# A fifth expert slot, laid over the modulated rows and their transposes, with the expert loop written out

## The reference, cut to what matters

```
e_w = e_prob / jnp.sum(e_prob, axis=-1, keepdims=True) * g_prob
combine = jnp.sum(jax.nn.one_hot(e_global, N_EXPERTS) * e_w[..., None], axis=1)
a = jnp.einsum('nd,edf->nef', t, w_g)        # 32 x 1024 x 256, f32
u = jnp.einsum('nd,edf->nef', t, w_u)        # 32 x 1024 x 256
act = jax.nn.silu(a) * u * combine[..., None]
y = jnp.einsum('nef,efd->nd', act, w_d)      # 32 x 256 x 1024
```

## Time and profile before

| what | value |
|---|---|
| median of the 3 runs | 1055.72 us (1053.0 to 1059.05) |
| the profiled execution, its own time | 1053.05 us |
| its span, first to last instruction | 1051.2 us |
| mean granted TensorE clock | 0.91 |
| PE busy | 832.2 us, 79% |
| DVE busy | 329.7 us, 31% |
| HBM traffic | 315.82 MB read, 26.80 MB written |

### The profile page before, as it was taken

One profiled execution on the slowest core, in us unless ns is written; L12 is line 12 of the kernel. 1 busy time (PEld: TensorE's weight loads), 2 busy tenths in 40 slices (PEclk: granted clock), 3 DMA queues, 4 the chain that ended last, 5 costly groups with the idle time before them and its releaser, 6 DMA issues.

```text
span 1051.2 us, 13810 instructions
## 1 busy us (share of the span) xinstructions
PE 832.2 (79%) x4921; PEld 438.8 (42%) x4922; DVE 329.7 (31%) x803; ACT 166.2 (16%) x354; POOL 159.0 (15%) x245
## 2 busy tenths in 40 slices
PE   3899999988976889787778937997599878797740
PEld 2556565655473333333323325664433323232310
DVE  3013555555852111111111147347411110111117
ACT  1122222242001011101111012201101111101110
POOL 1032030311102021111011101001201111111010
PEclk9999999999976999999889977998599998999985
DMA  9993653295397498999999889554569999999831
GB/s 337 365 361 109 217 175 125 81 360 206 92 398 321 178 370 334 419 420 420 419 420 396 329 301 375 194 207 183 227 273 419 420 421 421 419 413 418 357 132 72
DMA packets 90242, 318.11 MB, mean 303 GB/s; under 512 B 13150, under 2 KB 26174, under 8 KB 65624
## 3 DMA queue, kind: packets, MB, share of 16 engines
q1 hardware_dynamic: 70016, 274.60, 66.1%
q0 software_dynamic: 13376, 22.16, 6.1%
q10 hardware_dynamic: 6808, 20.79, 5.2%
HBM read 315.82 MB, written 26.80 MB: 326 GB/s over the span
## 4 chain that ended last, share of the span: by engine, by line
PE 48%; DMA 35%; DVE 8%; issue 4%; ACT 2%; SPq 2%; POOL 1%; ACTq 0%; DVEq 0%; POOLq 0%
DMA ring<-in_w_expert_up 24%; PE psum L919 16%; PE psum L802 8%; PE psum L748 7%; DMA ring<-in_w_ada 6%; PE psum L941 4%; PE psum L697 3%; DMA arena<-h_scratch,gidx 2%; PE psum L906 2%; DMA arena<-y_scratch 1%; PE psum L774 1%; SPq L366 1%; PE psum L1088 1%; PE psum L853 1%; PE psum L831 1%
## 5 line engine op out<-in xcount | busy, mean ns | idle before, releaser
L919 PE MATMUL psum<-ring,arena 128*64 128x512 f32 x1088 | 268.0, 649 | 54.6 <-DMA ring<-in_w_expert_up 50.6
L919 PEld LDWEIGHTS psum<-ring,arena 128*64 128x64 f32 x1088 | 95.0, 149 | 223.8 <-issue 221.7
L941 PE MATMUL psum<-ring,arena 128*64 128x512 f32 x544 | 124.2, 598 | 30.9 <-DVE arena L1663 29.5
L1659 DVE TENSOR_TENSOR arena<-arena,psum 128x256 f32<-128x256 f32 x34 | 14.3, 422 | 311.6 <-ACT arena L1212 311.6
L802 PE MATMUL psum<-ring,hT 128*128 128x384 f32 x288 | 97.9, 494 | 0.0
L941 PEld LDWEIGHTS psum<-ring,arena 128*64 128x64 f32 x544 | 39.7, 136 | 92.0 <-issue 76.6
L578 POOL DMA_INDIRECT y_scratch<-arena,sidx x34 | 34.5, 1014 | 255.3 <-DVE arena L1669 255.3
L748 PE MATMUL psum<-ring,hT 128*128 128x512 f32 x160 | 69.5, 593 | 1.1 <-ACT hT L1285 0.7
L697 PE MATMUL psum<-ring,silu 128*32 128x128 f32 x1536 | 52.7, 296 | 21.5 <-DMA ring<-in_w_ada 21.2
L802 PEld LDWEIGHTS psum<-ring,hT 128*128 128x128 f32 x288 | 54.3, 194 | 34.9 <-issue 1.4
L1669 DVE COPY arena<-psum 128x512 f32<-128x512 f32 x34 | 23.5, 692 | 132.6 <-PE psum L941 132.6
(11 more groups left out here) (177 smaller groups left out, 780.4 us busy)
## 6 DMA issues: line engine op xcount, KB each, us to landing
ring<-in_w_expert_gate SPq DMA_DIRECT2D x64, 1024.0 KB, 12.7
ring<-in_w_expert_up SPq DMA_DIRECT2D x64, 1024.0 KB, 19.5
ring<-in_w_expert_down SPq DMA_DIRECT2D x64, 1024.0 KB, 21.2
ring<-in_w_ada SPq DMA_DIRECT2D x24, 2048.0 KB, 15.7
ring<-in_w_qkv SPq DMA_DIRECT2D x9, 1024.0 KB, 12.4
arena<-m_scratch POOLq DMA_DIRECT2D x12, 512.0 KB, 7.4
h_scratch<-h ACTq DMA_DIRECT2D x6, 1024.0 KB, 10.6
arena<-y_scratch ACTq DMA_DIRECT2D x6, 1024.0 KB, 7.9
```

The source lines that it names most:

```text
L919: last = pe.matmul(bank[b][64 * e:64 * e + 64, :].rearrange("p (g n) -> p g n", g=2), mem.GT[b][:, c, 64 * e:64 * e + 64], w, start=(c == ...
L941: last = pe.matmul(bank[5 + half][64 * e:64 * e + 64, :], mem.actT[b][:, f, 64 * e:64 * e + 64], w[:, f, 512 * half:512 * half + 512], sta ...
```

## The change

`SLOTS` becomes 5. The ring keeps four slots; the fifth, `last_slot`, is one allocation in which `h` and `hT` lie side by side. Expert e goes to slot e modulo 5. The fifth slot's load (expert 4) is issued behind the loads of the first four, once the logits are done and `h_out` says that all rows are in HBM. After `gate_up` of pair n, SP now issues experts 2n + 5 and 2n + 6 (only expert 31 for n = 13). As the last pairs now sit in other slots, `ada` units 6 to 8, 10 and 11 of layer 1 move to A0 to A2, the second projection to B0 and B1, unit 9 to B2; and in layer 1 experts 2 and 3 are loaded first, 0 and 1 after the projection.

The loops over pairs are written out on all engines, so each has 16 copies of `first` and 16 of `body` per layer, and both packed words are read ahead of them. The gather and the `gt` past the end and the `landing` transfer are gone, and the fixed addresses no longer come from registers.

```
-SLOTS = 4
+SLOTS = 5
...
+SLOT_OF = [e % SLOTS for e in range(EXPERTS)]
...
-        self.ring = sb("ring", [P, SLOTS, SLOT])
+        self.ring = sb("ring", [P, (SLOTS - 1) * SLOT])
...
-        self.h = sb("h", [P, TILES, D])
-        self.hT = sb("hT", [P, KC, TOK])
+        self.last_slot = sb("h_hT", [P, SLOT])
+        self.h = self.last_slot[:, 0:TILES * D].rearrange("p (t n) -> p t n", t=TILES)
+        self.hT = self.last_slot[:, TILES * D:].rearrange("p (k n) -> p k n", k=KC)
...
+    def slot(self, e):
+        i = SLOT_OF[e]
+        return self.last_slot if i == SLOTS - 1 else self.ring[:, SLOT * i:SLOT * i + SLOT]
...
         def passes(eng, l, S, first, body):
-            eng.wait_ge(words_done, l + 1)
-            with eng.Fori(0, 2) as half:
-                word = eng.value_load(mem.words[0:1, bass.ds(half, 1)], min_val=0, max_val=(1 << 24) - 1)
-                with eng.Fori(0, PAIRS // 4) as it:
-                    for b in range(2):
...
+            word = words(eng, l)
+            for n in range(PAIRS):
+                first(n, n % 2)
+                times = times_of(eng, word, n)
+                with eng.If(times > 0):
+                    with eng.Fori(0, times) as r:
+                        body(n, n % 2, r + 1, eng.snap(further[eng]))
+                        eng.reg_add(further[eng], further[eng], 1)
...
+            def load_last_slot(l):
+                sp.wait_ge(logits_ps, l + 1)
+                sp.wait_ge(h_out, 16 * TILES * (l + 1))
+                load_expert(l, SLOTS - 1)
...
             for e in (2, 3):
                 load_expert(0, e)
+            load_last_slot(0)
...
+                for n in range(PAIRS):
...
+                    coming = [e for e in (2 * n + SLOTS, 2 * n + 1 + SLOTS) if e < EXPERTS]
+                    if coming:
+                        sp.wait_ge(main[l]["u_ps"], n + 1)
+                        sp.wait_ge(gate_up_through, all_done)
+                        for e in coming:
+                            load_gate_up(l, e)
+                        sp.wait_ge(main[l]["d_ps"], n + 1)
+                        sp.wait_ge(down_through, all_done)
+                        for e in coming:
+                            load_down(l, e)
...
-                    for e in range(2):
+                    for e in (2, 3):
                         load_expert(1, e)
                     sp.wait_ge(proj_ps, 12)
-                    for e in range(2, 4):
+                    for e in (0, 1):
                         load_expert(1, e)
+                    load_last_slot(1)
...
-                pool.dma_start(mem.landing[l:l + 1, :], A["k_rows"][0:1, 0:P]).then_inc(S["scattered"], 16)
...
-                    gt(S, n + 1, 16 * it + (16, 32)[b], 1 - b)
+                    if n + 1 < PAIRS:
+                        gt(S, n + 1, 16 * ((n + 1) // 2 + 1), 1 - b)
```

More of the change, by code:

```diff
@@ L68 @@
     LANDED[_unit] = _sum[_place]
+SLOT_OF = [e % SLOTS for e in range(EXPERTS)]
+LOAD_OF = {}
+for _l in range(2):
+    for _e, _s in enumerate(SLOT_OF):
+        LOAD_OF[_l, _e] = _l * SLOT_OF.count(_s) + SLOT_OF[:_e + 1].count(_s)
 _C = {}
@@ L436, in _ @@
                 load_expert(0, e)
+            load_last_slot(0)
             for l in range(2):
-                sp.wait_ge(words_done, l + 1)
-                for half in range(2):
-                    word = sp.value_load(mem.words[0:1, half:half + 1], min_val=0, max_val=(1 << 24) - 1)
-                    with sp.Fori(0, PAIRS // 4 - half) as it:
-                        for b in range(2):
-                            n = half * (PAIRS // 2) + it * 2 + b
-                            times = sp.snap((word >> (it * 6 + 3 * b)) & 7, min_val=0, max_val=PASSES - 1)
-                            first_done = sp.snap(n + 1)
-                            sp.reg_add(further[sp], further[sp], times)
-                            all_done = sp.snap(further[sp])
-                            slots = [2 * b + e for e in range(2)]
-                            experts = [sp.snap(2 * n + 4 + e) for e in range(2)]
-                            sp.wait_ge(main[l]["u_ps"], first_done)
-                            sp.wait_ge(gate_up_through, all_done)
-                            for e in range(2):
-                                load_gate_up(slots[e], l, experts[e])
-                            sp.wait_ge(main[l]["d_ps"], first_done)
-                            sp.wait_ge(down_through, all_done)
-                            for e in range(2):
-                                load_down(slots[e], l, experts[e])
@@ L671, in _ @@
-                pool.wait_ge(S["scattered"], 16 * PAIRS + 16)
+                pool.sem_inc(S["o_free"], 2)
+                word = words(pool, l)
+                for n in range(PAIRS):
+                    b = n % 2
+                    times = times_of(pool, word, n)
+                    pool.wait_ge(S["gt_ps"], n + 1)
+                    with pool.If(times > 0):
+                        gather(extra, l, PAIRS + n, pool.snap(further[pool]), 2)
+                    if n + 2 < PAIRS:
+                        gather(S, l, n + 2, n + 2, b)
+                    if n >= 1:
+                        pool.wait_ge(S["scattered"], 16 * n)
+                        pool.sem_inc(S["o_free"], 1)
+                    scatter(S, l, n, n, b)
+                    with pool.If(times > 0):
+                        pool.wait_ge(S["scattered"], 16 * n + 16)
+                        with pool.Fori(0, times) as r:
+                            k = pool.snap(further[pool])
+                            k16 = pool.snap(16 * k + 16)
+                            with pool.If(r > 0):
+                                gather(extra, l, (r + 1) * PAIRS + n, k, 2)
+                            pool.sem_inc(extra["o_free"], 1)
+                            scatter(extra, l, (r + 1) * PAIRS + n, k, b)
+                            pool.wait_ge(extra["scattered"], k16)
+                            pool.sem_inc(turns, 1)
+                            pool.reg_add(further[pool], further[pool], 1)
@@ L939, in down @@
                         for e in range(2):
-                            w = mem.ring[:, slots[e], 4 * D:].rearrange("p (k n) -> p k n", k=2)
+                            w = mem.slot(2 * n + e)[:, 4 * D:].rearrange("p (k n) -> p k n", k=2)
                             last = pe.matmul(bank[5 + half][64 * e:64 * e + 64, :],
@@ L947, in mlp, with first @@
                 S = main[l]
[L949 to L953 removed]
+                def first(n, b):
+                    pair = (2 * n, 2 * n + 1)
+                    gate_up(S, n, n, [(landed[SLOT_OF[e]], 32 * LOAD_OF[l, e]) for e in pair])
+                    if n + 1 < PAIRS:
+                        gt(S, n + 1, 16 * ((n + 1) // 2 + 1), 1 - b)
                     act_transposes(S, n, b)
[L955 removed]
+                    down(S, n, n, [(down_landed[SLOT_OF[e]], 16 * LOAD_OF[l, e]) for e in pair])
                 def body(n, b, r, k):
[L958 to L960 removed]
+                    pe.wait_ge(S["gt_act"], min(n + 2, PAIRS))
+                    pe.wait_ge(S["gt_dve"], min(n + 2, PAIRS))
                     gt(extra, k, 16 * k + 16, 2)
[L962 removed]
+                    gate_up(extra, k, n, [])
                     act_transposes(extra, k, b)
@@ L965, in body @@
                     pe.wait_ge(S["o_dve"], n + 2)
-                    down(extra, k, b, slots, [])
+                    down(extra, k, n, [])
                 gt(S, 0, 16, 0)
```

120 lines of the change are left out of this document (41 added, 79 removed).

## The result

The changed kernel takes 1042.62 us, median of four runs (1041.58 to 1043.62); the kernel before takes 1054.36 us in the runs beside it. The ratio is 0.9902 with a 95% interval of 0.9877 to 0.9928, so 8 to 13 us are gone. The profiled execution took 1042.36 us (span 1040.5) against 1053.05 (1051.2): 10.7 us less, where I had forecast 8.4.

What follows compares the result with a forecast made beforehand. Bytes through a full DMA queue at 420 GB/s were taken to bound both expert stages. Layer 0's -5.05 and layer 1's -3.35 us made -8.4, from the 1055.72 us median to 1047.3 us; range 1041 to 1056 us.

Steps and rivals of the forecast that it cites:

- What bounds it: Both expert stages: the DMA queue is full, so bytes at 420 GB/s set the pace and TensorE has slack.
- The fifth slot, -5.0 us per layer: Expert plateaus: one gate and one up load less ahead of the last gate-up block, 2.50 us each.
- The first gather, +1.0 us: Start of layer 1's expert stage: the added load delays the first gather by 1.0 us, between nothing and 2.7 us.
- half of what is left: Layer 1's first gather: queues alternate, so it waits a fair share of the load's remaining 2.7 us, taken as 1.0.
- Code, +1.0 us per layer: Expert stages: written-out TensorE code needs 12.8 more fetches per layer, spread evenly over 16 DMA engines, costing 1.0 us.
- the rival with one DMA engine behind by 11 us per layer: Expert stages: all added code fetches fall on one DMA engine, 16 us of its time per layer; slower, chance 0.09.
- The rival's second road: Each pair's `If`: a taken branch outside resident code fetches first; must exceed a few us of load wait; no separate chance.
- The `gt` past the end, -0.35 us per layer: Last pair of each layer: dropping VectorE's needless copy saves 0.35 us, between zero and 0.69 us.
- Between the layers, -0.7 us: Layer 0's end: one expert issue less ahead of the `ada` loads beside the last scatter, worth 0 to 2.5 us.
- my own signs of being wrong: Time wrong if first-to-last gate-up interval grows, layer 1's first gather far exceeds 4.4 us, or last blocks take 8.7.
- Given back by the clock and the gather: Two slow last blocks cost 3.4 us and the gather 2.0 instead of 1.0: 1051.7 us, chance 0.19.
- Less lag: Stage ends: the slowest DMA engine holds up the last block 2.5 us less per layer: 1042.3 us, chance 0.08.

Runs made afterwards that it cites:

- e4: Changed kernel with two more never-entered copies of the overflow pass in TensorE's code for each pair: 1075.50 us, 1.0222 of the kernel before.
- e1: Changed kernel with four slots and the old order of places and loads, loops still written out: 1049.39 us, 0.9961 of the kernel before.
- e2: Changed kernel with the fifth slot's load (expert 4) issued only after gate-up of pair 0: 1050.23 us, 0.9963 of the kernel before.
- e6: e1 with two gathers per layer and one `gt` past the end put back: 1051.52 us, 0.9985 of the kernel before.
- e7: Changed kernel with one more never-entered copy of the overflow pass in TensorE's code for each pair: 1043.04 us, 0.9900 of the kernel before.
- a2: Changed kernel run and profiled again, nothing altered: 1043.11 us, 0.9908 of the kernel before.
- e5: Changed kernel with gate and up of expert 31 queued ahead of expert 30's down matrix in each layer: 1039.43 us, 0.9873 of the kernel before.

## Why the prediction came out right

**What bounds it** held. Both expert stages are timed by bytes. The distance follows the bytes that stand in the queue ahead of pair 14's block and nothing else that I varied there, save e4's code.

**The fifth slot, -5.0 us per layer:** 4.8 us in layer 1 and 5.0 in layer 0 (e1 against after). The working, one gate and one up less ahead of the last block, is borne out from the other side by e2: a whole expert put back on the plateau costs 7.2 us.

**The first gather, +1.0 us:** it was 2.1 to 2.4. The bounds of 0 and 2.7 us held, but not "half of what is left". The load started at 737.88 us instead of the 746.6 that I worked out: the whole of layer 1 came some 8 us sooner, and its loads with it. Shifted by that it is 746.0, as forecast, and the gather's issue moved with it. So the overlap was as I had it, and what was wrong is the share of it that I gave to the gather.

**Code, +1.0 us per layer:** this term failed in size. 54 fetches were forecast as about 53; their price is zero within the ruler's 0.4 us. The 16-engine share of fetches vanished, and the rival with one DMA engine behind by 11 us per layer did not happen. The rival's second road, the stall at a jump, exists (e4), though not at this kernel's length of jump, where I had left it as part of a 0.09.

**The `gt` past the end, -0.35 us per layer:** from the last block's start to `down`'s, less the block's own length, the pair after is 0.25 us shorter in layer 0 and 0.27 in layer 1. The forecast was near.

**Between the layers, -0.7 us:** about -2 in the profiles of the result. Of it 0.9 us is the scatter, the place that I had named; that fewer load bytes beside it are the reason fits e1 and e6 (5.78 and 5.83 us) but was not tested by itself. The read of `y_scratch`, which I had not named, is 1.2 us shorter in the written-out form (e6) and long again in e7, but in this execution the load behind it gave that back. The 1.6 us of the two blocks behind the load are luck.

**The sum.** -8.4 forecast, -10.7 measured in the profiled executions. Of my terms, code gave 2.0 us too much cost, the gather 1.2 us too little, the space between the layers 1.3 us too little gain. The last block ran at the lower clock level for part of its time and took back 1.7 us, a risk that I had put into the range; the two shorter blocks between the layers (1.6 us, part of the space between them), a shorter tail and an earlier start of layer 0 come from nothing in the change that I can name.

In medians e1 makes the same cut without single executions. The terms of the form (code, `gt`) summed to +1.3 us and measured about -4; the terms of the slot (plateau, gather, scatter) summed to -9.7 and measured about -6. The mechanism of the slot was right, but both halves missed by 4 to 5 us with opposite signs, and that the total came out near is luck. The form's gain is 2 to 6 us by e1's interval; what makes it stays open beyond the 0.25 us per layer of the `gt`. Also, 1047.3 us stood on a median of 1055.72 us; in the runs beside the result the kernel before has 1054.36.

Two of my own signs of being wrong appeared: the first gather took 5.53 us, much over 4.4, and the last block of layer 1 took 8.78 us, over 8.7. The other signs came as forecast: 27 gate loads after 763 us, 54 packets on q8, no copy at the old line 1654 in the last pair. The last blocks start 5.7 and 5.1 us earlier relative to the first, where I had said 4 and 3.

**The rivals.** "Given back by the clock and the gather" had both of its pieces in part: the gather did cost over 2.0 us, and one of the two last blocks was slow in the first profile (none in a2's layer 1). It would have given 1051.7 us, in part because it kept the 2.0 us for code that were never there. "Less lag" names 1042.3 us, next to the 1042.62 measured, but no profile shows it: pair 14 came earlier by what the bytes give, and the stretch from pair 14 to pair 15 is the same within 0.3 us before and after, in each layer. Nor is the last wait a matter of lag alone: e5 shortens this stretch by 2.1 us in layer 1 with the same bytes.

## What to carry to other kernels

A buffer slot is worth the bytes that it lets go out in time in which DMA is idle, divided by the plateau's rate, less what the early load disturbs: look for every idle stretch before the plateau, and count how many issues the last consumer still has in front of it. At the end of a full queue the order of the last loads matters as well: one 1 MB load out of the way let the last block start 2.1 to 2.5 us sooner per layer in e5. Put what the last block waits for ahead of what it needs only later. Before writing a loop out, look at how many instructions a jump that is usually taken passes over, not only at how many bytes of code there are.

## What the runs showed of the hardware

**Code has a step, not a slope.** 27 fetches, 54 and 70 give the same plateau in layer 1 to 0.4 us at an equal number of slots; 85 fetches, with 348 instructions jumped per pair, cost 32 us, with waits of up to 3.4 us on "issue". Whether the jump or the fetches make the step was not separated.

**A wait and the block behind it.** In the rows above, blocks of 32 matmuls that waited 0.37 or 0.82 us took 7.09 us, and those that waited 2.83 to 3.44 us took 8.78 or 9.78 for the same work; a stretch of exactly one block of 8.78 us shows a granted clock of 0.80, so part of it ran at 1.2 GHz. The wait alone doesn't decide. TensorE in order of time, pair 15 of layer 0 of the changed kernel:

```profile
586.42 7.09 PE L926 MATMUL psum<-ring,arena 128*64 128x512 f32 x32 [2.43 <-DMA ring<-in_w_expert_up]
```

It waited 2.43 us and was fast; what else it takes stays open. The loads' pace hides the difference while pairs wait for bytes; only where no load is waited for, as at the end of a stage, does it show in the time.

**A short gather is dear beside a full queue.** The same gather takes 3.34 to 3.43 us with no load beside it and 5.5 to 5.8 us with the end of one.
